# Picking stage of a decoder layer: scaled one-hots on GpSimd, turned one-hots shared by ScalarE and VectorE, four cast buffers, first operands in U's ring

## The reference, cut to what matters

```
u   = take(u_tab, experts)                 # 128 rows of 2048 for each token
act = gelu(einsum("cd,ced->ce", x, u))     # one number for each pick
vv  = take(v_tab, experts)
out = einsum("ce,ced->cd", gates * act, vv)
```

## Time and profile before

| what | value |
|---|---|
| runs | 2193.90, 2198.16, 2200.42 us |
| profiled execution | 2197.67 us, span 2195.9 us |
| TensorE | 2111.8 us busy, 96% |
| VectorE | 1506.6 us, 69% |
| ScalarE | 1022.0 us, 47% |
| GpSimd | 420.6 us, 19% |
| DMA | 458.20 MB, 209 GB/s over the span |
| picking stage | from 1510.9 us (last matmul of U) to 1659.8 us (first of V) |

### The profile page before, as it was taken

One profiled execution on the slowest core, in us unless ns is written; L12 is line 12 of the kernel. 1 busy time (PEld: TensorE's weight loads), 2 busy tenths in 40 slices (PEclk: granted clock), 3 DMA queues, 4 the chain that ended last, 5 costly groups with the idle time before them and its releaser, 6 DMA issues.

```text
span 2195.9 us, 36752 instructions
## 1 busy us (share of the span) xinstructions
PE 2111.8 (96%) x14776; PEld 1970.4 (90%) x14776; DVE 1506.6 (69%) x2266; ACT 1022.0 (47%) x1524; POOL 420.6 (19%) x447
## 2 busy tenths in 40 slices
PE   7999999999899999999999999998989999999997
PEld 7999999889679999999999999998977888888886
DVE  5646556464644378886766667745876888888887
ACT  5434343333635444444444444443985444444443
POOL 1000000000000000000002222200113665666664
PEclk9999999999999999999999999999999999999998
DMA  7513132212455555665558888864886999999996
GB/s 241 164 37 108 46 102 66 87 49 78 163 182 183 173 176 184 183 184 183 185 179 259 279 269 277 272 204 154 276 301 231 323 321 322 326 335 338 332 337 237
DMA packets 148666, 458.20 MB, mean 209 GB/s; under 512 B 19825, under 2 KB 28033, under 8 KB 147729
## 3 DMA queue, kind: packets, MB, share of 16 engines
q1 hardware_dynamic: 114624, 342.94, 48.4%
q0 software_dynamic: 33872, 112.91, 14.9%
HBM read 426.34 MB, written 29.43 MB: 208 GB/s over the span
## 4 chain that ended last, share of the span: by engine, by line
PE 84%; DVE 8%; DMA 4%; ACT 2%; issue 2%; SPq 0%; DVEq 0%; ACTq 0%; POOLq 0%
PE ps L1469 84%; DMA jcast<-jrow_spill 2%; DVE lo L926 2%; DVE L L1111 1%; DMA oneI<-oneI_spill 1%; DMA x_sb<-in_x 0%; DVE xc L934 0%; DVE oneJT L931 0%; ACT oneG L845 0%; DVE ps L1389 0%; ACT hi L590 0%; DVE Tm L1123 0%; DVE TT L1117 0%; DVE wgt L1395 0%; ACT x_sq L602 0%
## 5 line engine op out<-in xcount | busy, mean ns | idle before, releaser
L1469 PE MATMUL ps<-hT_hi,hi 128*128 128x256 f32 x2992 | 854.6, 286 | 3.6 <-DVE rkv L934 3.6
L1469 PE MATMUL ps<-hT_lo,hi 128*128 128x256 f32 x2992 | 848.3, 284 | 0.0
L1469 PE MATMUL ps<-hT_hi,lo 128*128 128x256 f32 x2992 | 848.1, 283 | 0.0
L926 DVE TENSOR_TENSOR lo<-raw,hi 128x1024 fp32r<-128x1024 f32 x406 | 492.0, 1224 | 324.9 <-ACT hi L590 320.1
L590 ACT ACTIVATE hi<-raw 128x1024 fp32r<-128x1024 f32 x406 | 423.4, 1056 | 473.6 <-DMA raw<-in_peer_u 386.5
L1469 PEld LDWEIGHTS ps<-hT_hi,hi 128*128 128x128 f32 x2992 | 576.0, 193 | 5.7 <-DVE rkv L934 4.2
L1469 PEld LDWEIGHTS ps<-hT_lo,hi 128*128 128x128 f32 x2992 | 576.0, 193 | 0.1
L1469 PEld LDWEIGHTS ps<-hT_hi,lo 128*128 128x128 f32 x2992 | 575.8, 192 | 0.0
L554 POOL DMA_INDIRECT got<-in_peer_v,row_ids x256 | 317.4, 1240 | 220.8 <-DVE ps L934 145.0
L835 ACT ACTIVATE vhi<-vraw 128x1024 fp32r<-128x1024 f32 (+1 forms) x256 | 209.7, 843 | 279.8 <-DMA vraw<-in_peer_v 271.3
L1371 DVE TENSOR_TENSOR vlo<-vraw,vhi 128x1024 fp32r<-128x1024 f32 (+1 forms) x256 | 245.1, 959 | 72.3 <-ACT vhi L835 65.6
(11 more groups left out here) (275 smaller groups left out, 2094.2 us busy)
## 6 DMA issues: line engine op xcount, KB each, us to landing
raw<-in_peer_u SPq DMA_DIRECT2D x256, 512.0 KB, 4.3
vraw<-in_peer_v SPq DMA_DIRECT2D x128, 512.0 KB, 6.2
raw<-in_w_in SPq DMA_DIRECT2D x86, 512.0 KB, 3.6
vraw<-in_peer_v SPq DMA_DIRECT2D x128, 256.0 KB, 5.8
raw<-in_w_out SPq DMA_DIRECT2D x32, 512.0 KB, 3.7
raw<-in_wq SPq DMA_DIRECT2D x32, 512.0 KB, 3.6
oneJ_spill<-madeJ POOLq DMA_DIRECT2D x64, 256.0 KB, 4.8
oneJ<-oneJ_spill SPq DMA_DIRECT2D x64, 256.0 KB, 4.8
```

What stands on the lines that cost most here:

```text
L926: V.tensor_tensor(lo[n % NR][:, :], raw[n % NR][:, :], hi[n % NR][:, :].bitcast(F32), ALU.subtract).then_inc(lo_done, 1)
L1469: return nc.tensor.matmul(o, lhsT, rhs, start=start, stop=stop, skip_group_check=True)
```

## The change

*scaled* moves from ScalarE to GpSimd, as one multiplication of the whole group of four tokens with `wgt` spread along the free axis. Of the turned one-hots VectorE keeps those of even groups; ScalarE makes those of odd groups with two activations, |j - p| and then relu(1 - that). Both have semaphores of their own. There are four cast buffers instead of two. They, the first two turned one-hots (`first_jt`) and the first four `oneI` (`first_i`) lie in buffers of U's ring, so that they can be filled while the last two tiles of U are still multiplied. The loads of `oneI` are numbered anew: in step s SyncE does `load_one_i(s + 4)`, and then `load_one_j(s - 6)` as before. The first pieces of V are split after the loop's step 65 instead of from step 60 (ScalarE) and 64 (VectorE).

```diff
+N_FIRST, N_CAST = 4, 4
...
+        slots = [(2 * T_V - back) % NR for back in (5, 4)]
+        first_jt = [at(f"first_jt{i}", [P, TOK4, P], F32, raw_at + 4096 * slots[1] + 2048 * i)
...
             def load_one_i(g):
 
-                if g >= N_ONEI:
+                if g < N_FIRST:
+                    sync.dma_start(first_i[g][:, :, :].rearrange("p t i -> p (t i)"),
+                                   oneI_dram[g]).then_inc(sem(f"firstI_in{g}"), 16)
+                    return
+                if g >= N_FIRST + N_ONEI:
                     sync.wait_ge(sem("oneG_made"), g - N_ONEI + 1)
...
+            sync.wait_ge(mm_done, 2 * T_V - 4)
+            for g in range(N_FIRST):
+                load_one_i(g)
             sync.wait_ge(mm_done, 2 * T_V)
             for s in range(N_TOK4 + S_LAG - 2):
-                if s < N_TOK4:
-                    load_one_i(s)
+                if N_FIRST <= s + N_FIRST < N_TOK4:
+                    load_one_i(s + N_FIRST)
                 if s >= S_LAG - 2:
                     load_one_j(s - S_LAG + 2)
...
             def cast_rows(c):
 
-                if c < 2:
-                    pool.wait_ge(mm_done, 2 * T_V)
+                if c < N_CAST:
+                    pool.wait_ge(mm_done, 2 * T_V - 4 + c // 2)
                 else:
-                    pool.wait_ge(sem("oneJT_made"), BC_TOK // TOK4 * (c - 1))
+                    for q in range(2):
+                        pool.wait_ge(sem(f"oneJT_made{q}"), c - N_CAST + 1)
...
+            def scaled(g):
+
+                pool.wait_ge(sem("w_done"), g // 4 + 1)
+                if g >= 2:
+                    pool.wait_ge(sem("gates_made"), g - 1)
+                wait_one_i(pool, g)
+                nc.gpsimd.tensor_tensor(
+                    oneG[g % 2][:, :, :], one_i(g)[:, :, :],
+                    wgt[:, TOK4 * g:TOK4 * g + TOK4].unsqueeze(2).broadcast_to([P, TOK4, P]),
+                    ALU.mult).then_inc(sem("oneG_made"), 1)
...
-            for c in range(N_BC):
+            for c in range(N_CAST):
                 cast_rows(c)
+            for s in range(1, N_TOK4 + 7):
+                if s % 2 and N_CAST <= (s + 7) // 2 < N_BC:
+                    cast_rows((s + 7) // 2)
+                if s >= 7:
+                    scaled(s - 7)
...
+            def one_hot_jt(g):
+
+                wait_jcast(act, g)
+                if g < 2:
+                    act.wait_ge(mm_done, 2 * T_V - 3)
+                else:
+                    act.wait_ge(sem("picks_out"), g - 1)
+                nc.scalar.activation(one_jt(g)[:, :, :], cast_tokens(g), ACT.Abs, bias=minus_p).then_inc(
+                    sem("far_made"), 1)
+                act.wait_ge(sem("far_made"), g // 2 + 1)
+                nc.scalar.activation(one_jt(g)[:, :, :], one_jt(g)[:, :, :], ACT.Relu, scale=-1.0,
+                                     bias=one_c).then_inc(sem("oneJT_made1"), 1)
...
             for s in range(N_TOK4 + S_LAG + 1):
+                if s % 2 == 0 and s + 1 < N_TOK4:
+                    one_hot_jt(s + 1)
...
-                if 7 <= s < N_TOK4 + 7:
-                    scaled(s - 7)
                 if s > S_LAG:
                     gates_in(s - S_LAG - 1)
-                if 60 <= s < 60 + 2 * V_HIS:
-                    v_hi(s - 60)
+                if s == 65:
+                    act.wait_ge(sem("oneJT_made0"), N_TOK4 // 2)
+                if 65 <= s < 65 + 2 * V_HIS:
+                    v_hi(s - 65)
...
-                if s + 1 < N_TOK4:
+                if s % 2 and s + 1 < N_TOK4:
                     one_hot_jt(s + 1)
...
-                if 64 <= s < 64 + 2 * V_HIS:
-                    v_lo(s - 64)
+                if s >= 66:
+                    v_lo(s - 66)
```

More of the change, by code:

```diff
@@ L326, in hybrid_layer_kernel @@
         oneJT = [at(f"oneJT{i}", [P, TOK4, P], F32, raw_at + 65536 + 2048 * i) for i in range(2)]
-        jcast = [at(f"jcast{i}", [P, BC_TOK, P], BF16, raw_at + 69632 + 2048 * i) for i in range(2)]
+        slots = [(2 * T_V - back) % NR for back in (5, 4)]
+        first_jt = [at(f"first_jt{i}", [P, TOK4, P], F32, raw_at + 4096 * slots[1] + 2048 * i)
+                    for i in range(2)]
+        first_i = [at(f"first_i{i}", [P, TOK4, P], BF16, raw_at + 4096 * slots[0] + 1024 * i)
+                   for i in range(N_FIRST)]
+        jcast = [at(f"jcast{i}", [P, BC_TOK, P], BF16,
+                    raw_at + 4096 * (NR + slots[i // 2]) + 2048 * (i % 2)) for i in range(N_CAST)]
         a_hi = [at(f"a_hi{i}", [P, 4, SEQ], F32R, raw_at + 43008 + 4096 * i) for i in range(2)]
@@ L350, in gate_bank, with one_i, one_jt, wait_one_i @@
             return ps[:, 2 + g % 3]
+        def one_i(g):
+            return first_i[g] if g < N_FIRST else oneI[g % N_ONEI]
+        def one_jt(g):
+            return first_jt[g] if g < 2 else oneJT[g % 2]
+        def wait_one_i(eng, g):
+            if g < N_FIRST:
+                eng.wait_ge(sem(f"firstI_in{g}"), 16)
+            else:
+                k = g % N_ONEI
+                eng.wait_ge(sem(f"oneI_in{k}"), 16 * (g // N_ONEI + (1 if k >= N_FIRST else 0)))
+        def wait_jcast(eng, g):
+            c = g * TOK4 // BC_TOK
+            eng.wait_ge(sem(f"jcast_in{c % N_CAST}"), 16 * (c // N_CAST + 1))
+        def cast_tokens(g):
+            return jcast[g * TOK4 // BC_TOK % N_CAST][:, TOK4 * g % BC_TOK:TOK4 * g % BC_TOK + TOK4]
         def sum_bank(t):
@@ L371, in hybrid_layer_kernel @@
         eps_c, gneps_c, ssq8 = scal[:, 46:47], scal[:, 47:48], scal[:, 48:56]
-        p_number = scal[:, 56:57]
+        p_number, minus_p, one_c = (scal[:, 56 + i:57 + i] for i in range(3))
         omu, oka, psp = idxT[:, 0, 0:27], idxT[:, 0, 32:40], idxT[:, 0, 40:48]
@@ L532, in cast_rows @@
             def cast_rows(c):
-                if c < 2:
-                    pool.wait_ge(mm_done, 2 * T_V)
-                else:
-                    pool.wait_ge(sem("oneJT_made"), BC_TOK // TOK4 * (c - 1))
-                pool.dma_start(jcast[c % 2][:, :, :].rearrange("p t e -> p (t e)"),
+                if c < N_CAST:
+                    pool.wait_ge(mm_done, 2 * T_V - 4 + c // 2)
+                else:
+                    for q in range(2):
+                        pool.wait_ge(sem(f"oneJT_made{q}"), c - N_CAST + 1)
+                pool.dma_start(jcast[c % N_CAST][:, :, :].rearrange("p t e -> p (t e)"),
                                jrow_dram[c * BC_TOK:(c + 1) * BC_TOK].rearrange(
                                    "t e -> (t e)").partition_broadcast(P)).then_inc(
-                    sem(f"jcast_in{c % 2}"), 16)
+                    sem(f"jcast_in{c % N_CAST}"), 16)
+            def scaled(g):
[7 more added lines that the diff above has]
+                    ALU.mult).then_inc(sem("oneG_made"), 1)
             v_rows = a["peer_v"].rearrange("i j (q d) -> (i j q) d", d=DS)
@@ L861, in weights_turned @@
                     sem("wT_in"), 1)
+            act.wait_ge(sem("p_made"), 1)
             for s in range(N_TOK4 + S_LAG + 1):
+                if s % 2 == 0 and s + 1 < N_TOK4:
+                    one_hot_jt(s + 1)
                 if s % 4 == 1 and 5 <= s <= N_TOK4 + 1:
@@ L1341, in _ @@
                                         scalar=0.0, op0=ALU.mult, op1=ALU.add, accum_out=p_number))
+            link(ts(minus_p, p_number, -1.0, None, ALU.mult))
+            V.memset(one_c, 1.0).then_inc(sem("p_made"), 1)
             def one_hots(g):
@@ L1374, in one_hot_jt @@
             def one_hot_jt(g):
-                c = g * TOK4 // BC_TOK
-                dve.wait_ge(sem(f"jcast_in{c % 2}"), 16 * (c // 2 + 1))
-                if g >= 2:
+                wait_jcast(dve, g)
+                if g < 2:
+                    dve.wait_ge(mm_done, 2 * T_V - 3)
+                else:
                     dve.wait_ge(sem("picks_out"), g - 1)
-                tok = slice(TOK4 * g % BC_TOK, TOK4 * g % BC_TOK + TOK4)
-                ts(oneJT[g % 2][:, :, :], jcast[c % 2][:, tok], p_number, None, ALU.is_equal).then_inc(
-                    sem("oneJT_made"), 1)
+                ts(one_jt(g)[:, :, :], cast_tokens(g), p_number, None, ALU.is_equal).then_inc(
+                    sem("oneJT_made0"), 1)
             def chosen(g):
                 dve.wait_ge(sem("picks_out"), g + 1)
-                dve.wait_ge(sem(f"oneI_in{g % N_ONEI}"), 16 * (g // N_ONEI + 1))
+                wait_one_i(dve, g)
                 pb = pick_bank(g).rearrange("p (t i) -> p t i", t=TOK4)
-                V.tensor_tensor(pb, pb, oneI[g % N_ONEI][:, :, :], ALU.mult).then_inc(
+                V.tensor_tensor(pb, pb, one_i(g)[:, :, :], ALU.mult).then_inc(
                     sem("picks_chosen"), 1)
@@ L1788, in picks @@
             def picks(g):
-                pe.wait_ge(sem("oneJT_made"), g + 1)
+                pe.wait_ge(sem(f"oneJT_made{g % 2}"), g // 2 + 1)
                 if g >= 3:
@@ L1793, in picks @@
                 for k in range(TOK4):
```

(2 more changed lines are left out.)

## The result

The changed kernel takes **2265.3 us** (median of 4 runs, 2264.6 to 2265.6) against 2198.3 before: ratio 1.0307, 95% interval 1.0289 to 1.0325, 3.1% slower. Forecast were 2258 us and a range of 2223 to 2297. The profiled execution took 2265.0 us, span 2263.2.

What follows compares the result with a forecast made beforehand. It took the order in SyncE's queue to decide, oneJ not issued before scaled(g) is done: 2197.7 - 6.2 (start) + 73.1 (middle) - 7.3 (end) = 2257.3, say 2258 us; range 2223 to 2297, 76%.

Steps and rivals of the forecast that it cites:

- The ring: Picking stage, groups 4 to 53: gates(g-2), scaled(g), issues of oneI and oneJ, landing, gates(g); 6.93 us per two groups, +73.1 us.
- scaling on GpSimd: In each round, GpSimd's product of one group: 1.25 us, bounds 0.689 and 2.48.
- landing of oneJ: In each round, oneJ from issue to landing: 3.5 us, bounds 2.6 and 4.8.
- clock: In each round, TensorE 55% busy may get the lower clock: 0.4 us added, bounds 0 and 0.8.
- heavy ring: Rival, 10%: scaling 2.48 or held off, landing 4.8 from step 44; round about 9 us, 2310 us, from 2297 on.
- Start: After U's last matmul: picks start some 0.8 us later instead of 5.3, gates(0) at 1524.3 instead of 1530.5: -6.2 us.
- End: Last ten gates, 54 to 63: ScalarE no longer binds, 1.3 us a group, 13 us instead of 20.3: -7.3 us.
- The way to V and V: The V stage behind the picking stage: same work, 0 us.
- Hidden terms: In the ring: ScalarE's one-hots 1.2 us a step, cast issue 0.538 us, VectorE's saved 0.24 us a step; all cost or gain 0.
- The light: Rival, 7%: scaling 0.7, landing 2.6, full clock; round 5.07 us, 2211 us, up to 2223.
- GpSimd alone: Rival, 3%: GpSimd binds at 2.75 us a step and the ring doesn't; 2222 us.
- TensorE's bound: Rival, 4%: the ring is slack and TensorE binds the middle at 1.79 us a step, 89.5 us; 2173 us, faster.

Runs made afterwards that it cites:

- experiment 1: The changed kernel with the old load order, oneI of group s loaded again in step s instead of s+4: 2187.2 us, ratio 0.9947.
- 2: The kernel before with only the first four oneI loaded ahead and oneI of group s+4 loaded in step s: 2261.4 us, ratio 1.0283.
- 3: The changed kernel with step s loading oneI of group s+3 instead of s+4: 2214.0 us, ratio 1.0067.
- experiment 6: The changed kernel with the casts of tokens 32 to 255 left out, so the output is not the reference's: 2235.7 us, ratio 1.0175.
- Experiment 8: The changed kernel with old load order, scaling on ScalarE, all turned one-hots on VectorE; early start and four cast buffers stay: 2191.8 us, ratio 0.9967.
- 11: The changed kernel with the old load order, four buffers oneG and the cast behind the scaling: 2196.0 us, ratio 0.9982.
- 4: The changed kernel with four buffers oneG instead of two, its load order kept: 2207.7 us, ratio 1.0046.
- 9: The changed kernel with four oneG, its load order kept, and VectorE's one-hot made against a PSUM column: 2212.1 us, ratio 1.0063.
- 10: The changed kernel with the old load order and VectorE's one-hot made against a PSUM column: 2185.8 us, ratio 0.9947.
- 12: The changed kernel with old load order, four oneG, the cast behind the scaling and VectorE's one-hot against a PSUM column: 2181.2 us, ratio 0.9931.

## Why the prediction was right

**The ring.** That oneJ of group g is behind scaled(g), that this closes a ring over two groups, that it holds for 50 groups: shown by SyncE's 50 waits, by experiment 1 (taking the order away takes 78 us away), by 2 (the order alone gives it) and by 3 (three groups in a round).

**The round's size** was 6.93 us in the forecast and 6.94 in the round shown; the mean over the middle is 172.8 / 25 = 6.91, with rounds from 5.7 to 8.0. The sum is better than its terms, and that is luck:

| term, us | forecast | trace |
|---|---|---|
| gates(g) first matmul to the scaling | 1.2 | 1.29 |
| scaling on GpSimd | 1.25 | 1.04 |
| to the issue of oneJ | 0.53 | 0.40 |
| landing of oneJ | 3.5 | 4.17 |
| TensorE wakes | 0.05 | 0.04 |
| clock | 0.4 | 0 in this round |

The landing was 0.7 too low. I had spread the cast's 256 KB over the round as thin traffic; it leaves at the same moment as the oneJ that counts, and costs 1.0 to 1.2 us there (experiment 6). The scaling was 0.2 too high, and so was the prediction's other estimate for it, 1.1 to 1.35 us, which came from a figure for an addition of f32 numbers. The clock was too high. Stretches of the changed kernel, the last three one round each (columns as in rows 2):

```profile
1580.00:1601.00 21.00, 11.52 (x96) 10.94 (x96) 9.26 (x16) 8.02 (x13) 7.78 (x9) 1.00 0.48 146
...
1602.48:1609.24 6.76, 5.47 (x33) 5.28 (x33) 2.94 (x6) 2.46 (x5) 2.59 (x3) 0.75 0.40 116
...
1649.84:1657.27 7.43, 3.84 (x33) 3.65 (x33) 3.07 (x5) 2.64 (x4) 2.59 (x3) 1.00 0.74 241
1657.27:1664.95 7.68, 5.46 (x32) 5.27 (x33) 3.11 (x6) 2.74 (x5) 2.59 (x3) 0.78 0.76 231
```

With 55% busy the clock stayed at its upper level of 2.4 GHz for three rounds in a row; in seven of the 25 rounds it was at its lower level for a part (0.73 to 0.80 in the mean of the round), and the mean of the middle is 0.93. Those seven took 7.14 us on average and the other 18 took 6.82, four of the seven less than 6.8: about 0.1 us a round over the whole middle, not 0.4. The longest stretch of long rounds has another mark. From 1649.84 to 1680.52 four of them took 7.43, 7.68, 8.03 and 7.54 us, two at full clock and two not; there SyncE loads V's first pieces in between, and the DMA engines are busy for 0.69 to 0.83 of the time. The prediction named this for its heavy ring; it held for four rounds, some 3 us in all. I read one fall of the clock at the end of the stage as a rule for half of the time. With the landing 0.7 too low, the scaling 0.2 and the clock 0.3 to 0.4 too high, wrong terms cancelled.

**Start**, -6.2 in the forecast, -3.3 measured. Picks did start at 1511.29. But gates(0) started at 1525.95 instead of 1524.3, for a reason that I had put aside in a sentence on GpSimd: VectorE's one-hot stood still beside the first two scalings, and TensorE waited 2.35 us for it.

```profile
1521.85 2.67 DVE L989 TENSOR_SCALAR oneJT<-jcast,scal 128x512 f32<-128x512 bf16 x1
1522.18 2.05 POOL L586 TENSOR_TENSOR oneG<-first_i,wgt 128x512 f32<-128x512 bf16 x2
...
1524.57 1.59 PE L1529 MATMUL ps<-Zq,oneJT 128*128 128x128 f32 x8 [2.35 <-DVE oneJT L989]
```

The rest was lost from gates(0) to the end of gates(3), which took 7.6 us (clock 0.83) where the kernel before took 6.4 at full clock:

```profile
1530.50:1536.90 6.40, 6.40 (x60) 6.40 (x59) 6.40 (x14) 5.17 (x16) 1.07 (x2) 1.00 0.66 206
```

The forecast had no term for the clock here. Experiment 8, with no scaling on GpSimd, gained 7.1 us by the end of gates(3).

**End**, -7.3 in the forecast, -3.6 measured: ScalarE no longer binds, but GpSimd's last scalings and VectorE's first differences of V stand in each other's way. GpSimd is busy for 13.6 of these 16.7 us, and three scalings take 5.5 us where three alone take 3.1:

```profile
1712.52 6.09 DVE L1431 TENSOR_TENSOR vlo<-vraw,vhi 128x1024 fp32r<-128x1024 f32 x4 [1.30 <-ACT vhi L888]
1712.55 5.51 POOL L586 TENSOR_TENSOR oneG<-oneI,wgt 128x512 f32<-128x512 bf16 x3 [0.37 <-PE ps L1529]
```

By the Trainium skill's rule on the shared port (SBUF — State Buffer, section Who interferes with whom) a VectorE instruction that uses both ports and a GpSimd one exclude each other for whole instructions; the trace agrees for the one-hot at the start, 2.67 us for 0.48 us of work with two scalings of together 2.05 us beside it. I had weighed it as a delay of the scaling within the round. It wasn't that: in the round the two rarely meet (mean of the one-hot 0.550 us), and where it met two scalings in a row it was VectorE that stood still. At the end of the stage the scaling was held up too.

**The way to V and V** stood at 0 in the forecast and took 1.6 us more; what made them longer was not looked into. So the 7.7 us by which the profiled executions differ more than forecast (67.3 against 59.6) are 2.9 from the start, 3.7 from the end, 1.6 from here and -0.5 from the middle.

**Hidden terms.** ScalarE's one-hots (two of 0.721 us each, forecast 0.6), the cast's issue and VectorE's saved half cost or gave nothing that can be seen in the round, as said. There was one table load.

**Rivals.** The light and the heavy ring were 7 and 10%; the changed kernel lies between them. The four rivals add up to 24%, not the 2 in 10 given with the range: GpSimd alone, at 2222 us, lies outside the range too. TensorE's bound, 2173 us, needed the ring to be slack: experiment 1, where it is, takes 2187, since the middle is 98 and not 89.5 us and the two ends gave 9 and not 13.5.

## What to carry to other kernels

Before a load is moved forward in an in-order queue, write down for each load behind it what the moved one waits for: a prefetch that has to wait for its buffer passes its wait on to everything behind it. If that wait hangs on the very step that the next load feeds, a latency that was hidden becomes a round, and its length divided by the number of groups in flight is the new step. An engine that takes over work for relief brings its queue and its ports along; measure it with the engine that will run beside it.

## What the runs showed of the hardware

- A GpSimd product of 128x512 (bf16 times f32) took 1.04 us alone, against 0.689 us for VectorE's product of that size.
- VectorE's comparison of 128x512 (tensor_scalar, input and output in SBUF) took 0.479 us alone, and in the mean 0.936 us in experiment 1, 1.37 in 11 and 1.73 in 4, where two of GpSimd's scalings often ran in a row beside it. As a tensor_tensor with its second operand in PSUM it took 0.676 to 0.677 us in experiments 9, 10 and 12, beside the same scalings.
- OneJ's 256 KB landed in 2.8 us with no casts (median, experiment 6) and in 4.2 us beside a cast (the round shown).
- The granted clock stayed at 1.00 for 21 us with TensorE busy for 55%, and fell to its lower level in parts of seven other rounds of the same make; what decides was not settled.
